# Delta rule with beta moved into the triangular solve, the decay's mask moved to GpSimd, and a new set of planner ranks

## The reference, cut to what matters

```
gc = cumsum(g)                       # log-decay inside a chunk
decay = exp(where(causal, gc[:, None] - gc[None, :], -inf))
a_mat = where(strict, beta[:, None] * (k @ k.T) * decay, 0)
t_mat = inverse(eye + a_mat)         # lower triangular
w_c = t_mat @ (beta * k * exp(gc)) ; u_c = t_mat @ (beta * v)
...                                  # scan over the chunks with a state
sink: softmax over [scores, sink], the sink's column dropped
```

## Time and profile before

| | before |
|---|---|
| median of 3 runs | 2294.95 us |
| lowest and highest run | 2293.42 and 2296.1 us |
| profiled execution: span, first to last instruction | 2291.9 us |
| profiled execution: its own time | not listed beside the span |
| TensorE matmul / weight load busy | 98% / 78% |
| VectorE / ScalarE / GpSimd busy | 70% / 49% / 45% |
| chain of work that ended last: TensorE / VectorE / ScalarE | 84% / 8% / 2% |

### The profile page before, as it was taken

One profiled execution on the slowest core, in us unless ns is written; L12 is line 12 of the kernel. 1 busy time (PEld: TensorE's weight loads), 2 busy tenths in 40 slices (PEclk: granted clock), 3 DMA queues, 4 the chain that ended last, 5 costly groups with the idle time before them and its releaser, 6 DMA issues.

```text
span 2291.9 us, 31262 instructions
## 1 busy us (share of the span) xinstructions
PE 2247.2 (98%) x11389; PEld 1785.5 (78%) x11389; DVE 1594.7 (70%) x2217; ACT 1112.9 (49%) x2008; POOL 1030.9 (45%) x643
## 2 busy tenths in 40 slices
PE   9999989999999999999999999999999999999999
PEld 6778867677878888887887777777777888888886
DVE  7865768776596554689449798888888655545745
ACT  5554157674364555444446365645433322225553
POOL 2212245444247666657767211111123765556663
PEclk9999999999999999999999999999999999999999
DMA  4113353344325443955452301111123343338554
GB/s 160 40 44 99 122 177 107 98 139 158 109 93 188 161 152 133 314 173 166 143 170 83 124 29 46 47 46 47 56 79 124 134 143 111 111 133 294 183 171 147
DMA packets 153764, 289.43 MB, mean 126 GB/s; under 512 B 34915, under 2 KB 44387, under 8 KB 153612
## 3 DMA queue, kind: packets, MB, share of 16 engines
q1 hardware_dynamic: 153612, 287.44, 38.3%
HBM read 207.88 MB, written 79.51 MB: 125 GB/s over the span
## 4 chain that ended last, share of the span: by engine, by line
PE 84%; DVE 8%; ACT 2%; issue 2%; DMA 2%; POOL 1%; SPq 0%; DVEq 0%; POOLq 0%; ACTq 0%
PE bank L869 12%; PE bank L871 12%; PE bank L867 12%; PE bank L639 12%; PE bank L643 11%; PE bank L641 11%; PE bank L716 2%; PE bank L932 2%; PE bank L963 1%; PE bank L945 1%; ACT t L1005 1%; DVE t L1434 1%; DVE t L1974 1%; PE bank L836 1%; PE bank L854 1%
## 5 line engine op out<-in xcount | busy, mean ns | idle before, releaser
L2100 POOL TENSOR_TENSOR t<-t,t 128x512 fp32r<-128x512 f32 (+1 forms) x494 | 810.5, 1652 | 1068.3 <-ACT t L1005 1062.1
L1005 ACT ACTIVATE t<-t 128x512 fp32r<-128x512 f32 (+1 forms) x689 | 448.3, 676 | 653.5 <-PE bank L871 276.3
L639 PE MATMUL bank<-t,t 128*128 128x512 f32 x1360 | 548.5, 403 | 0.0
L643 PE MATMUL bank<-t,t 128*128 128x512 f32 x1360 | 531.4, 391 | 1.1 <-DVE t L1434 0.6
L641 PE MATMUL bank<-t,t 128*128 128x512 f32 x1360 | 530.1, 390 | 1.7 <-POOL t L2100 1.7
L867 PE MATMUL bank<-t,t 128*128 128x512 f32 x1316 | 514.2, 391 | 6.2 <-DVE t L1818 4.6
L869 PE MATMUL bank<-t,t 128*128 128x512 f32 x1316 | 513.3, 390 | 1.4 <-POOL t L2100 1.4
L871 PE MATMUL bank<-t,t 128*128 128x512 f32 x1316 | 513.1, 390 | 0.7 <-DVE t L1434 0.7
L639 PEld LDWEIGHTS bank<-t,t 128*128 128x128 f32 x1360 | 255.7, 188 | 62.7 <-issue 12.7
L643 PEld LDWEIGHTS bank<-t,t 128*128 128x128 f32 x1360 | 255.3, 188 | 58.3 <-POOL t L2100 1.3
L641 PEld LDWEIGHTS bank<-t,t 128*128 128x128 f32 x1360 | 255.9, 188 | 56.3 <-issue 4.6
(11 more groups left out here) (250 smaller groups left out, 2641.2 us busy)
## 6 DMA issues: line engine op xcount, KB each, us to landing
t<-in_w SPq DMA_DIRECT2D x87, 512.0 KB, 3.6
hid_scr<-t SPq DMA_DIRECT2D x112, 256.0 KB, 2.1
t<-hid_scr SPq DMA_DIRECT2D x112, 256.0 KB, 2.7
t<-in_wf SPq DMA_DIRECT2D x80, 256.0 KB, 3.3
t<-in_wf SPq DMA_DIRECT2D x36, 512.0 KB, 4.5
g_scr<-t SPq DMA_DIRECT2D x36, 512.0 KB, 2.9
t<-g_scr SPq DMA_DIRECT2D x72, 256.0 KB, 3.4
t<-in_wo SPq DMA_DIRECT2D x24, 512.0 KB, 3.6
```

Source lines behind the costliest of these rows:

```text
L639: e.matmul(ps[:, :], hi[:, w, :], XH[:, x, hs], start=k == 0, stop=False)
L643: last = e.matmul(ps[:, :], hi[:, w, :], XL[:, x, hs], start=False, stop=k == j.nk - 1)
L1005: return e.activation(out, in_, ACT.Copy, **kw)
L2100: return e.tensor_tensor(out, x, high.bitcast(F32), ALU.subtract)
```

## The change

It has these parts. (1) beta goes on the right-hand side of the small solve (`zi` copies it to the diagonal of Z in place of ones), so that the joined inverse already holds it; `lmul` scales rows in both directions. (2) So `bel` and `a1` go, `kkl` loads k k^T straight into AT, for each unit on a semaphore of its own, and the tile kkL goes. (3) `ltt` is one unscaled copy at the top level too. (4) A new GpSimd step `dn` writes mask + own decay into D; `dd` then subtracts EB by a tensor_tensor, and `ebx` needs no bias and is one operation for D. (5) `as1` has two operations for three, with the negated sink made once in `gc`. (6) `SHIFT` is set anew: 162 entries, 13 of them for keys that it had before and 4 of these with the old value; `ss` waits for all readers of its buffer and each `sv` is ordered behind the last one.

```diff
-SHIFT = {("abias",): 1.5, ("apv", 1): 1.25, ("atr", 3): -1.5, ("bg", 1): -1, ("bm2", 0): -0.25, ("bm2", 1): 3, ("cR", 1): 1.75, ("co", 0, 4): -2,
...
+SHIFT = {("a2",): 2, ("abias",): 1.75, ("apv", 1): 0.5, ("apv", 5): -2, ("apv", 5, 0): 4.25, ("aqk", 5, 2): -3, ("aqk", 7, 1): -4, ("atc", 1, 4): 6.75,
...
     def ebx(d, i):
...
-        q.wait_ge(done("dd", d, i), done("gd"))
+        q.wait_ge(done("dd", d, i))
         e.activation(EB[:, :, :], EB[:, :, :], ACT.Exp, scale=-1.0).then_inc(*tick("ebx", d, i))
-        for j in range(4):
-            a = e.activation(D[:, j, :], D[:, j, :], ACT.Exp, bias=G["ngc"][:, n, 4 * d + j:4 * d + j + 1])
-        a.then_inc(*tick("ebx", d, i))
+        e.activation(D[:, :, :], D[:, :, :], ACT.Exp).then_inc(*tick("ebx", d, i))
...
-        if l < TOP:
-            a = copy(TT[:, :, :], v4(ps))
-        else:
-            for j in range(4):
-                a = copy(TT[:, j, :], ps[:, 128 * j:128 * j + 128], scale=G["beta"][:, n, 4 * d + j:4 * d + j + 1])
-        a.then_inc(*tick("ltt", d, i, l))
+        copy(M.unit(d, i, "TT")[:, :, :], v4(K.prep_bank("lx", d, i, l))).then_inc(*tick("ltt", d, i, l))
...
     def dd(d, i):
-        q.wait_ge(done("gcl", d, i), done("c1"))
-        if i >= 2:
-            q.wait_ge(done("lx", d, i - 2, TOP))
-        if i in (1, 2):
-            q.wait_ge(*[done(*x) for x in K.p1_x])
-        elif i == 0:
+        D = M.unit(d, i, "D")[:, :, :]
+        q.wait_ge(done("gcl", d, i), done("dn", d, i))
+        if i == 0:
...
-        stt(M.unit(d, i, "D")[:, :, :], M.unit(d, i, "EB")[:, :, :], -1.0, over_heads(C(f"neg{d}")), ALU.mult, ALU.add).then_inc(*tick("dd", d, i))
-
-    def a1(d, i):
-        AT = M.unit(d, i, "AT")[:, :, :]
-        q.wait_ge(done("kkl", d, i), done("bel", d, i))
-        tt(AT, AT, M.kkL[:, :, :], ALU.mult).then_inc(*tick("a1", d, i))
+        tt(D, D, M.unit(d, i, "EB")[:, :, :], ALU.subtract).then_inc(*tick("dd", d, i))
...
-        q.wait_ge(part("zi", (), 1))
+        q.wait_ge(part("zi", (), 1), done("gS", 0), done("gS", 1))
         for d in range(2):
-            last = e.memset(M.Z[:, d].rearrange("p a b -> p (a b)")[:, 0:1024:33], 1.0)
+            last = e.tensor_copy(M.Z[:, d].rearrange("p a b -> p (a b)")[:, 0:1024:33], M.gS[:, d, 0, :])
...
     def a2(d, i):
...
-        q.wait_ge(done("ebx", d, i), done("a1", d, i))
+        q.wait_ge(done("ebx", d, i), done("kkl", d, i))
...
-        q.wait_ge(done("rows"))
-        tt(sm[:, :, 8:12], sm[:, :, 0:4], sink, ALU.max).then_inc(*tick("as1", n))
+        q.wait_ge(done("rows"), done("gc"))
+        stt(sm[:, :, 12:16], sm[:, :, 0:4], -1.0, below, ALU.mult, ALU.min).then_inc(*tick("as1", n))
         q.wait_ge(part("as1", (n,), 1))
-        ts(sm[:, :, 12:16], sm[:, :, 8:12], -1.0, None, ALU.mult)
-        tt(sm[:, :, 16:20], sink, sm[:, :, 8:12], ALU.subtract).then_inc(*tick("as1", n))
+        tt(sm[:, :, 16:20], sink, sm[:, :, 12:16], ALU.add).then_inc(*tick("as1", n))
...
+    def dn(d, i):
+
+        n = i if d == 0 else 7 - i
+        mask, own = C(f"neg{d}").unsqueeze(1).broadcast_to([128, 4, 128]), M.G["ngc"][:, n, 4 * d:4 * d + 4].unsqueeze(2).broadcast_to([128, 4, 128])
+        q.wait_ge(done("gd"), done("c1"))
+        if i >= 2:
+            q.wait_ge(done("lx", d, i - 2, TOP))
+        elif i == 0:
+            q.wait_ge(*([done("inv_out")] if d else [done("whi", 22), done("wlo", 22)]))
+        if i in (1, 2):
+            q.wait_ge(*[done(*x) for x in K.p1_x])
+        e.tensor_tensor(M.unit(d, i, "D")[:, :, :], mask, own, ALU.add).then_inc(*tick("dn", d, i))
...
+            add("sp", "kkl", d, i, rank=r + PREP_RANK.get((d, i), 0))
+            add("pool", "dn", d, i, rank=r - 1)
...
-            add("pe", "sv", i, p_, rank=3)
+            add("pe", "sv", i, p_, rank=3, behind=[("sv", K.piece_before(12 * i + p_, 1))] if i or p_ else ())
```

More of the change, by code:

```diff
@@ L1506, in lmul @@
         q.wait_ge(done("lex", d), done("gS", d))
[L1507 removed]
+        tt(L, L, beta.unsqueeze(2).broadcast_to([128, 32, 32]), ALU.mult).then_inc(*tick("lmul", d))
         q.wait_ge(part("lmul", (d,), 1), *[done("kk_in", n) for n in range(8)])
@@ L1981, in ss @@
             i0, p0 = K.piece_before(n, 2)
-            q.wait_ge(done("st", i0, PIECES[p0][0], (PIECES[p0][2] - 1) // 256))
+            q.wait_ge(*[done("st", i0, PIECES[p0][0], g) for g in range(PIECES[p0][1] // 256, (PIECES[p0][2] + 255) // 256)])
         stt(w, x, -1.0, ps[:, 0:nk], ALU.mult, ALU.add).then_inc(*tick("ss", a, i, p_))
@@ L2087, in ofd @@
         tt(M.xr[:, m, :], M.xr[:, m, :], M.OF[:, m, :], ALU.add).then_inc(*tick("ofd", h, m))
-    return dict(pads=pads, idle=idle, nacc=nacc, x1l=x1l, cv=cv, kn=kn, ga=ga, gc=gc, gd=gd, lmul=lmul, zi=zi, sol=sol, zt=zt, dd=dd, a1=a1, a2=a2, qkm=qkm, lp=lp, lt=lt, cr=cr, cO=cO, cs=cs,
+    return dict(pads=pads, idle=idle, nacc=nacc, x1l=x1l, cv=cv, kn=kn, ga=ga, gc=gc, gd=gd, lmul=lmul, zi=zi, sol=sol, zt=zt, dd=dd, a2=a2, qkm=qkm, lp=lp, lt=lt, cr=cr, cO=cO, cs=cs,
                 gn=gn, am=am, as1=as1, as2=as2, ao=ao, yal=yal, zm=zm, gg=gg, evd=evd, hac=hac, hac2=hac2, x2l=x2l, xn=xn, tx=tx, tl=tl, ws=ws, fu2=fu2, fu3=fu3, fc11=fc11, fu4=fu4, fc22=fc22, fc21=fc21, fc12=fc12, ft3=ft3, ft2=ft2,
@@ L2369, in gcl, with kkl @@
         start(flat(M.unit(d, i, "EB")[:, :, :]), M.row_of(64 + 8 * n + 4 * d), "gcl", d, i)
-    def bel(d, i):
+    def kkl(d, i):
         n = i if d == 0 else 7 - i
-        q.wait_ge(done("gT_out"))
+        q.wait_ge(done("kk_out", n))
         if i >= 2:
@@ L2379, in bel @@
             q.wait_ge(*([done("inv_out")] if d else []), done("whi", 21), done("wlo", 21))
-        start(flat(M.unit(d, i, "AT")[:, :, :]), M.row_of(8 * n + 4 * d), "bel", d, i)
-    def kkl(d, i):
-        n = i if d == 0 else 7 - i
-        q.wait_ge(done("kk_out", n))
-        if (d, i) != (0, 0):
-            q.wait_ge(done("a1", *((0, i) if d else (1, i - 1))))
-        start(flat(M.kkL[:, :, :]), M.kk_scr[n], "kkl", d, i)
+        start(flat(M.unit(d, i, "AT")[:, :, :]), M.kk_scr[n], "kkl", d, i)
     def qk_out(d, i):
@@ L2876, in signals @@
     g["gcl"] = lambda d, i: f"d_gc{d}{i % 2}"
-    g["bel"] = lambda d, i: f"d_be{d}{i % 2}"
-    g["kkl"] = "d_xl0"
+    g["kkl"] = lambda d, i: f"d_kk{d}{i % 2}"
     g["qk_out"] = lambda d, i: f"d_wb{i}" if d == 0 else f"d_blk{4 + i}"
@@ L2892, in signals @@
     return g
-PARTS = dict(mp=0, fsq=2, wc=2, nr=2, kr=2, gb=5, ebx=2, gr=2, fr=2, qx=2, na=2, nc=2, gq=2, se=2, cv=4, gc=5, gd=2, lmul=2, sol=2, lex=2, zi=2, ge=2, kk_in=4, gS=2, inv_out=4, inv_in=2, as1=2, as2=2, cz=3, pf=2, ss=3)
+PARTS = dict(mp=0, fsq=2, wc=2, nr=2, kr=2, gb=5, ebx=2, gr=2, fr=2, qx=2, na=2, nc=2, gq=2, se=2, cv=4, gc=6, gd=2, lmul=2, sol=2, lex=2, zi=2, ge=2, kk_in=4, gS=2, inv_out=4, inv_in=2, as1=2, as2=2, cz=3, pf=2, ss=3)
 PARTS["or"] = 2
@@ L2975, in first_layer @@
             add("sp", "gcl", d, i, rank=r + PREP_RANK.get((d, i), 0))
-            add("sp", "bel", d, i, rank=r + PREP_RANK.get((d, i), 0))
+            add("sp", "kkl", d, i, rank=r + PREP_RANK.get((d, i), 0))
+            add("pool", "dn", d, i, rank=r - 1)
             add("dve", "dd", d, i, rank=r + PREP_RANK.get((d, i), 0))
@@ L2979, in first_layer @@
             add("pool", "sc", d, i, rank=r)
-            add("dve", "a1", d, i, rank=r + PREP_RANK.get((d, i), 0))
             before = [("lx", (d, i - 2, TOP))] if i >= 2 else [("lb", (0, 0, TOP)), ("lb", (1, 0, TOP))] if i else []
-            add("sp", "kkl", d, i, rank=r + PREP_RANK.get((d, i), 0))
             add("dve", "a2", d, i, rank=r + PREP_RANK.get((d, i), 0))
```

22 lines of the change are left out of this document (13 added, 9 removed), and 25 rows, old and new, of tables (SHIFT, SIGNALS).

## The result

The changed kernel takes **2317.85 us** (median of 4 runs, 2311.5 to 2319.87) against 2294.77 us before in the same session: a ratio of 1.0094 [1.008, 1.0108], so **23 us slower** where 2286 was forecast, and outside the whole range of 2272 to 2298. The profiled execution took 2317.62 us with a span of 2315.8; that is 1.8 us for what lies around the span. Two executions of the experiments, 2450 us of `edits_no_ranks` and 2800 us of `beta_part_order_kept`, ran at a far lower clock, and the ratios leave them out.

The account below looks back on a forecast made before the run. Large matmuls bound most of the kernel; the delta rule and attention stage held 28.1 us to gain. Terms -2 -4 -1 -1 -1.5 +0.5 made -9 us, so 2294.95 became 2286 us; own range 2279 to 2290, whole range 2272 to 2298.

Parts of the forecast that it names:

- the ranks: Planner's ties in all queues: -4 us behind the projections, -1 for other stage waits, -1.5 at 655 us.
- the second rival: Whole kernel: all is hidden beside busy TensorE, new ties open as many gaps as they close; about 2294, chance 0.18.
- dd and dn: Delta rule: dd at most +3.8 us on VectorE, new dn +19.3 us on GpSimd; +0.5 us in the sum.
- the third rival: Delta rule: dn waits in GpSimd's queue or holds VectorE, 1.38 us each time; 2305 at all 14 units, chance 0.16.
- GpSimd's hold on VectorE: Delta rule and attention: new GpSimd operations hold VectorE ones, +4 us of VectorE, ends 0 and 19.3.
- my balance: Delta rule and attention, busy times forecast: VectorE 164 us, ScalarE 142, GpSimd 132, TensorE as before.
- a1, zi, the plain ltt and as1: a1 gone -2 us; zi 0; ltt with ebx -1; as1 shortens attention's path by about 0.2 us a block.
- ebx: Delta rule, one piece for four: ScalarE saves 9.0 us, each unit's path 0.64; with ltt -1 us in the sum.
- The opening wait: TensorE's 5.2 us wait behind the projections, with 1.7 us of clock: -4 of these 6.9 us.
- The wait at 655 us: Wait of 4.6 us where the feed-forward starts, with 2.7 us of clock: -1.5 of 7.3 us.
- dd's form: Delta rule, scalar_tensor_tensor to tensor_tensor: mean 0.744 to 1.015 us, at most +3.8 us on VectorE.
- No engine becomes the bound: Delta rule and attention: with VectorE at 164 us, ScalarE 142 and GpSimd 132, each queue has more air.

Follow-up runs that it names:

- edits_no_ranks: All edits of the change with an empty table of ranks, against the kernel before: 2323.9 us, ratio 1.0124.
- beta_part_order_kept: Only the edits of beta, ltt and as1, old dd and ebx, no dn, queues in the order of before: 2293.2 us, ratio 0.9992 to before.
- the chain cut: All edits in the order of before, dn writing a spare tile so that it need not wait for lx: 2293.1 us, ratio 0.9988 to before.
- edits_order_kept: All edits of the change, each queue in the order of the kernel before: 2305.7 us, ratio 1.0045 to before.
- beta_new_order: Only the edits of beta, ltt and as1, decay as before, no dn, in the changed kernel's order: 2313.2 us, ratio 1.0072 to before.
- the decay's part: Old code with only dn, the new dd and ebx, in the order of before: 2311.4 us, ratio 1.0067 to before.

## Why the prediction was wrong

**The sign was wrong because of two of its steps.** The first is "the ranks". I wrote that they "decide ties only", took -4, -1 and -1.5 us for them, and the worst that I allowed the new ties was "as many gaps as they close", in the second rival. The order in fact costs 12.3 us outside the stage and 13.3 inside it, against the order of before with the chain cut. I had looked at where before had waits that a new order could close, and not at the 1758 us and 306 us where there was almost nothing to win and all to lose. That "a new wait elsewhere may eat it" stood there without a price. The warning that I gave, "a first stage that ends later than 306 us", did come: it ends at 313.3. So did "a stage of 228 us or more" and "VectorE groups whose means have grown".

**The second is "dd and dn", +0.5 us.** "It needs no load and can run ahead of gcl" left out that `dn` writes D, which `lx` of two units before must have read; I named that wait in the third rival and put no price on it. What I priced was occupation: 1.38 us an operation, and a hold of VectorE. Measured: `dn` 1.07 us, occupation within the measurement's error, blocking 1.9 to 3.9, and 12.6 in all for `dn` between `lx` and `dd` in the order of before. The third rival had the right side and nearly the right place ("in GpSimd's in-order queue it waits for the transposed inverse"), but its time, 2305, rests on 1.38 us for each `dn` and not on the waits. That `edits_order_kept` also gives 2305.7 is a coincidence of sums.

**A term that was too small** is GpSimd's hold on VectorE: I took +4 us of VectorE's time and no cost from it. In the kernel after, four untouched groups take 14.4 us more, and VectorE has 176.8 us where my balance said 164. `beta_new_order` shows that the order brings it and not `dn`.

**Part by part.** *a1, zi, the plain ltt and as1:* forecast -2 and part of the -1, measured -1.8 us for them together, in the order of before (just within no change). *ebx:* 9.0 us less of ScalarE (17.9 became 8.9), as worked out; with the decay's part as a whole at a loss, no gain of it shows, and it was not run apart. *The opening wait:* the longest went from 5.19 to 2.16 us. In the first 20 us behind the projections TensorE is idle 5.9 us for 7.7 (before, 306 to 326 us), and the clock is 1.00 for 0.83, which is 3.4 us of work. That is -5.2, but 5.1 us of work were lost to the clock right behind, at 333 to 353 us. Over the first 40 us it has issued 274 matmuls for 272, so nothing is left of the -4. *The wait at 655 us:* it went, and one of 5.1 us came at 645, so the -1.5 was a move and no gain. *dd's form:* 0.21 us above the mean that I took, at most 3 us of VectorE. *No engine becomes the bound:* right, and beside the point. What moved the time was who stands behind whom in five queues.

**What stays open.** Which swaps of two steps inside the stage cost the 13 us, and which of the others cost the 12.3, was not tried one by one. The waits of L852 for L1629, of L683 for its input and of L877 for L1432 are where the loss shows; that they are its cause is argued from the traces only. How the 12.6 us divide between `dn`'s wait for `lx` and its place in GpSimd's queue is open, and so is what VectorE's 14 us cost. `kkl` for each unit was not tried apart from beta's part either.

## What to carry to other kernels

When an operation goes to another engine, write down what its output tile must wait for and which queue will do that waiting: a tile that a third engine still reads turns two parallel waits into a chain, and one spare tile (here 2 KB a partition) was worth 12.6 us where the operation itself was free. In an in-order queue the operation then stands behind other work too. A tie-break table is part of the code it was fitted to; hold the order of every queue fixed to price an edit, then price the order by itself and by place, outside the edited stage too. Where the kernel is 98% full, a new order has little to win and much to lose.

## What the runs showed of the hardware

Sixteen more GpSimd operations of about 1.1 us beside a VectorE that is 72% busy changed no time that 10 runs of each kernel could tell (0.9992 for 0.9992), although single VectorE operations do stretch. Another order of the same operations did change it: with no `dn` at all, VectorE's busy time in the stage went from 158.9 to 173.6 us, in groups that read tiles alone, while those that read a bank stayed as they were. And the clock can cost as much as the waits: of the 9.5 us by which the stage of `edits_order_kept` is longer, up to 6.8 are work lost at the lower level, and no view of waits shows it. With the chain cut, the windows from 420 to 470 us are at 1.00, where the kernel before had 0.97.
